# Adaptive modulation products regrouped, and RMS norms applied after the products, in a four-layer fp32 stack

## The reference, cut to what matters

```python
def _rms_norm(x, gain):
    xf = x * lax.rsqrt(jnp.mean(x * x, axis=-1, keepdims=True) + NORM_EPS)
    return xf * gain

def first_block(x, ...):                      # two layers, 512 tokens
    for layer in range(2):
        hn = _rms_norm(x, norm_mix_pre[layer])
        mix = _sparse_attn_conv_mixer(hn, ...) if layer == 0 else _mla_mixer(hn, ...)
        x = x + _rms_norm(mix, norm_mix_post[layer])
        hn = _rms_norm(x, norm_ffn_pre[layer])
        x = x + _rms_norm(jnp.square(jax.nn.relu(hn @ mlp_w1[layer])) @ mlp_w2[layer], norm_ffn_post[layer])

def adaln(cvec, w, b):                        # w is 1024 x 3072
    return jnp.split(jax.nn.silu(cvec) @ w + b, 3, axis=-1)

def second_block(x, c, ctx, c_ctx, ...):      # two layers, 512 + 256 tokens
    for i in range(2):
        shift, scale, gate = adaln(c, mod_w[i], mod_b[i])
        shift_c, scale_c, gate_c = adaln(c_ctx, mod_w[i], mod_b[i])
        u_lat = rms_norm(h_lat, norm_g[i]) * (1.0 + scale) + shift
        u_ctx = rms_norm(h_ctx, norm_g[i]) * (1.0 + scale_c) + shift_c
        ...                                   # i = 0 differential attention, i = 1 neighbourhood attention
        h_lat = h_lat + gate * out_l          # and h_ctx + gate_c * out_c after i = 0
```

## Time and profile before

| | |
|---|---|
| median of 3 runs | 4143.25 us (4135.88 to 4145.75) |
| profiled execution | 4144.13 us, span 4142.5 us |
| PE / DVE / ACT busy | 93% / 50% / 27% of the span |
| mean granted TensorE clock | 0.959 |
| modulation products (L1466) | 768 instructions, 136.2 us |
| MLP products (L456) | 3584 instructions |

### The profile page before, as it was taken

The page is one execution under the profiler, slowest core; times in us unless marked ns, Lnnn a source line. Parts: engine busy times, 40 slices in busy tenths (PEclk is TensorE's granted clock), DMA queues, the critical chain, the costliest instruction groups (busy, mean ns, idle before and its releaser), DMA issues. The chain is left out here.

```text
span 4142.5 us, 44540 instructions
## 1 busy us (share of the span) xinstructions
PE 3833.1 (93%) x16250; PEld 2479.6 (60%) x16250; DVE 2058.4 (50%) x3726; ACT 1136.8 (27%) x2079; POOL 142.6 (3%) x227
## 2 busy tenths in 40 slices
PE   6998999998889999999999999999697999999989
PEld 2445688874445888866565656565354555555554
DVE  3743453533553635446666666666303555555540
ACT  1112100011331000103343444434100444444430
POOL 6500000000000000000000000000000000000000
PEclk8998899987998999889999999999899999999999
DMA  7521323321013332421010111111011121111111
GB/s 151 138 71 46 102 76 97 82 77 48 22 46 88 90 91 72 107 77 36 26 32 29 30 30 30 30 30 31 15 51 46 48 56 56 56 56 56 56 41 53
DMA packets 456432, 246.26 MB, mean 59 GB/s; under 512 B 44256, under 2 KB 448352, under 8 KB 456320
## 3 DMA queue, kind: packets, MB, share of 16 engines
q1 hardware_dynamic: 420384, 216.15, 18.8%
q0 software_dynamic: 14144, 28.36, 2.6%
q10 hardware_dynamic: 21792, 0.22, 0.4%
HBM read 229.83 MB, written 14.80 MB: 59 GB/s over the span
## 5 line engine op out<-in xcount | busy, mean ns | idle before, releaser
L1152 PE MATMUL bank<-hT,ring 128*128 128x512 f32 (+1 forms) x1664 | 634.0, 531 | 23.4 <-DVE hT L1527 19.8
L1628 PE MATMUL bank<-hT,ring 128*128 128x512 f32 (+1 forms) x1536 | 521.1, 491 | 21.0 <-DVE big L1880 16.3
L1152 PEld LDWEIGHTS bank<-hT,ring 128*128 128x128 f32 x1664 | 310.8, 191 | 300.8 <-issue 269.5
L1628 PEld LDWEIGHTS bank<-hT,ring 128*128 128x128 f32 x1536 | 287.4, 190 | 250.3 <-issue 212.5
L326 PE MATMUL bank<-big,ring 128*128 128x512 f32 (+1 forms) x1024 | 391.9, 546 | 12.1 <-DVE big L1892 8.4
L326 PEld LDWEIGHTS bank<-big,ring 128*128 128x128 f32 x1024 | 196.7, 192 | 206.0 <-issue 185.5
L1057 ACT ACTIVATE arena<-bank 128x512 f32<-128x512 f32 (+2 forms) x224 | 118.3, 528 | 461.7 <-PE bank L1050 461.6
L456 PE MATMUL bank<-big,arena 128*128 128x256 f32 x1024 | 228.8, 379 | 0.0
L456 PEld LDWEIGHTS bank<-big,arena 128*128 128x128 f32 x1024 | 194.6, 190 | 26.5
L1025 DVE CUSTOM_DVE_ANT_0 arena<-bank,big 128x512 f32<-128x512 f32 (+2 forms) x152 | 101.3, 666 | 199.7 <-PE bank L1005 199.7
L1623 PEld LDWEIGHTS bank<-ring,hT 128*128 128x128 f32 x1536 | 177.7, 192 | 30.4 <-DVE arena L1847 17.0
(11 more groups left out here) (278 smaller groups left out, 5515.4 us busy)
## 6 DMA issues: line engine op xcount, KB each, us to landing
ring<-in_mlp_w SPq DMA_DIRECT2D x128, 512.0 KB, 5.2
ring<-in_a_w_in SPq DMA_DIRECT2D x64, 512.0 KB, 4.0
ring<-in_b_w_in SPq DMA_DIRECT2D x64, 512.0 KB, 4.0
ring<-in_mod_w SPq DMA_DIRECT2D x48, 512.0 KB, 3.7
ring<-in_even_w_in SPq DMA_DIRECT2D x32, 512.0 KB, 4.0
bias_d<-tb POOLq DMA_DIRECT2D x96, 128.0 KB, 3.4
big<-bias_d POOLq DMA_DIRECT2D x16, 768.0 KB, 5.4
ring<-in_a_w_out SPq DMA_DIRECT2D x16, 512.0 KB, 3.7
```

Of the source, the lines that this page charges most:

```text
L1152: mm = pe.matmul(bk(b + n)[0:m, 0:z - a], ring[s][:, k, 0:m], (rhs or hcol)(k, a, z), start=k == 0, stop=k == kt - 1)
L1628: mm = pe.matmul(flatb[2][:, a:z], ring[s][:, k, :], hT[:, k, a:z], start=k == 0, stop=k == KT - 1)
```

## The change

1. **Modulation.** `cc` grows to 32 columns (30 of zeros) and becomes the stationary operand; four slabs move at a time, each to its own 32 columns of the array and its own 32 partitions of bank 5. 48 blocks are dealt as 8, 4, 4, 8 in each half: 8 in each residual stage, 4 each at steps 7 and 13 of each MLP. The result is copied (`dve_mod_copy`), turned by a transpose (`pe_mod_turn`) and added to the bias (`dve_mod_add`).
2. **Residual stages.** ACT writes `hT = xT * gain` tile by tile behind DVE's additions, and the squares go to another buffer. The reciprocal of the second root moves behind the start of the products.
3. **MLP.** C11, C12 and C21/C22 are evacuated by DVE as `max(x, 0) * rs`, and ACT squares them. `u2` comes ahead of S1 and S2, and S3 ahead of the four differences in an `up` step.
4. **`low`.** DVE evacuates with `* rs`; tables are made behind the second product; the first latent's sums and scaling come behind its own products.
5. **Second block.** The context half is normed in `mlp1` (residual 2 covers 768 tokens, residual 3 only 512) and its shift is on ACT; the latent half is handed over tile by tile, its shift on ACT. The first product of `dif` and of `nat` waits for each tile.
6. **Norm 9.** DVE adds the squares in `wout2`, PE sums once. The first two groups of `nat` start on latent and context halves apart.

```diff
-        MODS = [0, 11, 22, 33, 48]
+        MODS = [("mod0", 0, 8, 0), ("modx0", 8, 4, 0), ("mody0", 12, 4, 4), ("mod1", 16, 8, 0),
+                ("mod2", 24, 8, 0), ("modx1", 32, 4, 0), ("mody1", 36, 4, 4), ("mod3", 40, 8, 0)]
+        MOD_STEP = {7: 1, 13: 2}
-                    mm = pe.matmul(bk(5)[:, 2 * n:2 * n + 2], ring[s][:, k, :], cc[:, k, :],
-                                   start=k == 0, stop=k == KT - 1, skip_group_check=True)
-                mm.then_inc(slab_done[s], 1)
+                    for j in range(4):
+                        mm = pe.matmul(bk(5)[32 * j:32 * j + 32, P * q:P * q + P], cc[:, k, :],
+                                       ring[s0 + 4 * q + j][:, k, :], start=k == 0, stop=k == KT - 1,
+                                       skip_group_check=True)
+                        if k == KT - 1:
+                            mm.then_inc(slab_done[s0 + 4 * q + j], 1)
+            dve.tensor_copy(mod_raw[:, 0:32 * blocks], bk(5)[:, 0:32 * blocks]).then_inc(md_r, 1)
+                m = pe.transpose(bk(5)[:, C + P * q:C + P * q + P], mod_raw[:, P * q:P * q + P], ident)
...
         def sp_mlp(sp, mlp):
             for st in mlp.steps:
+                if st.s - 1 in MOD_STEP:
+                    sp_mod(sp, 4 * mlp.i + MOD_STEP[st.s - 1])
...
         def pe_mlp(pe, mlp):
+                if s == 2:
+                    pe_mod_turn(pe, 4 * mlp.i)
+                if s in MOD_STEP:
+                    pe_mod(pe, 4 * mlp.i + MOD_STEP[s])
+                if s - 1 in MOD_STEP:
+                    pe_mod_turn(pe, 4 * mlp.i + MOD_STEP[s - 1])
...
         def act_mlp(act, mlp):
+                if s == 4 and mlp.i == 1:
+                    act_shifted(act, 0, 1)
-                    act.wait_ge(m_prod, mlp.past("prod") + 7 * s + P2)
-                    act.activation(c11, st.C, ACT.Relu).then_inc(m_c11, 1)
+                    act.wait_ge(m_c11, mlp.past("c11") + s + 1)
+                    act.activation(kept(B11, st.j), c11, ACT.Square).then_inc(m_b, 1)
+                    act.activation(b12, c12, ACT.Square).then_inc(m_b, 1)
+                    act.wait_ge(m_c2, mlp.past("c2") + u + 1)
+                    act.activation(pair, c2.rearrange("p (a n) -> p a n", a=2), ACT.Square).then_inc(m_b, 1)
...
         def dve_mlp(dve, mlp):
             weights(first, S3)
+            dve_rs(dve, mlp.pre, mlp.c)
...
+                done(P6)
+                dve.wait_ge(m_copied, mlp.past("copied") + 2 * s + 1)
+                dve.tensor_tensor(u2, p1s[e], st.X, ALU.add).then_inc(m_u2, 1)
                 if nxt:
                     weights(nxt, S1)
                     weights(nxt, S2)
+                if s == 2:
+                    dve_mod_add(dve, 4 * mlp.i)
+                if s == 3 and mlp.i == 1:
+                    dve_modulated(dve, 0, 1)
+                if s in MOD_STEP:
+                    dve_mod_copy(dve, 4 * mlp.i + MOD_STEP[s])
+                if s - 1 in MOD_STEP:
+                    dve_mod_add(dve, 4 * mlp.i + MOD_STEP[s - 1])
-                    dve.wait_ge(m_c11, mlp.past("c11") + s + 1)
-                    dve.tensor_tensor(kept(B11, j), c11, c11, ALU.mult).then_inc(m_b, 1)
+                    dve.scalar_tensor_tensor(out=c11, in0=st.C, scalar=0.0, in1=rs[:, 0:H],
+                                             op0=ALU.max, op1=ALU.mult).then_inc(m_c11, 1)
...
+            for k in range(KT):
+                act.wait_ge(r_x, KT * r.i + k + 1)
+                if g_pre is not None:
+                    act.activation(hT[:, k, 0:S], xT[:, k, 0:S], ACT.Copy, scale=gains[:, g_pre, k:k + 1])\
+                        .then_inc(n_out, 1)
+                act.activation(sqr[:, k, 0:S], xT[:, k, 0:S], ACT.Square).then_inc(n_sq, 1)
...
-            if g_pre is not None:
-                dve_rs(dve, r.pre, c)
-                dve_scaled(dve, xT, gains[:, g_pre, :], hT, c)
+            dve_mod_copy(dve, (0, 3, 4, 7)[r.i])
...
+                dve.tensor_tensor(lat[:, n, :], bk(n % 2), rs[:, 0:S], ALU.mult).then_inc(l_raw, 1)
+                if n == 1:
+                    dve_tables(dve, tab1, 1)
+                if n == 4:
+                    scaled(0, 0, 3)
...
+        def act_shifted(act, layer, c):
+                act.wait_ge(u_t, base + k + 1)
+                act.activation(hT[:, k, a:z], hT[:, k, a:z], ACT.Identity, bias=mods[:, layer, k, c:c + 1])\
+                    .then_inc((n_out, u_c)[c], 1)
...
+            dve_gated_squares(dve, gated2, pre9)
+            dve_rs(dve, pre9, S)
+            dve_modulated(dve, 1, 0)
+            dve.reciprocal(rs[:, S:TT], rs[:, S:TT]).then_inc(n_rs, 1)
+            dve.wait_ge(n_rs, pre9.i + 2)
+            dve_modulated(dve, 1, 1)
             dve_nat(dve)
```

More of the change, by code:

```diff
@@ L652, in dve_mlp @@
                     dve.tensor_tensor(half_sum[tb_][:, 0:H], u3, st.Z, ALU.subtract).then_inc(m_free, 1)
-                if nxt:
+                if nxt and not st.up:
                     weights(nxt, S3)
@@ L1470, in dve_mod_out @@
[L1470 to L1478 removed]
+            phase, n0, blocks, s0 = MODS[b]
@@ new lines, in dve_mod_copy, with pe_mod_turn @@
+        def dve_mod_copy(dve, b):
+            phase, n0, blocks, s0 = MODS[b]
+            if b == 0:
+                dve.wait_ge(b_w, 16 * 8 * 12)
+            for s in range(blocks):
+                multiplied(dve, phase, s0 + s, 0)
+            dve.tensor_copy(mod_raw[:, 0:32 * blocks], bk(5)[:, 0:32 * blocks]).then_inc(md_r, 1)
+        def pe_mod_turn(pe, b):
+            pe.wait_ge(md_r, b + 1)
+            for q in range(MODS[b][2] // 4):
+                m = pe.transpose(bk(5)[:, C + P * q:C + P * q + P], mod_raw[:, P * q:P * q + P], ident)
+            m.then_inc(md_t, 1)
@@ L1624, in project @@
                                            start=k == 0, stop=k == KT - 1, skip_group_check=True)
+                elif x == "q" and h is None:
+                    for c, (a, z) in enumerate(spans(TT)):
+                        if c:
+                            pe.wait_ge(u_c, KT)
+                        for k in range(KT):
+                            if c == 0:
+                                pe.wait_ge(n_out, res3.pre.k + k + 1)
+                            mm = pe.matmul(flatb[2][:, a:z], ring[s][:, k, :], hT[:, k, a:z],
+                                           start=k == 0, stop=k == KT - 1)
                 else:
@@ L2339, in _ @@
             act_std(act, pre9, TT, 6)
+            act_shifted(act, 1, 0)
+            act_shifted(act, 1, 1)
             run_pairs(nat, "act", act)
```

266 lines of the change are left out of this document (145 added, 121 removed).

## The result

The changed kernel takes 4002.56 us, the median of 4 runs (4002.36 to 4011.99), against 4143.56 (4135.88 to 4145.75): a ratio of 0.9668, 95% interval 0.9650 to 0.9687. That is 141 us less. The profiled execution took 4011.99, span 4010.3; the other three have spans of 4000.7 to 4000.9. The steps are compared by the profiled pair, spans 4142.5 and 4010.3.

A forecast was written before the change was run, and what follows sets the result against it. TensorE, busy 93% of the span, was taken as the bound, with stages one behind another so savings add. Terms -20, -42, -19, -31, -17 and +13 sum to -116 us, taking 4144.1 to 4028; 8-in-10 range 4008 to 4070.

The forecast's parts named there:

- +13: Both MLPs together: 13 us added by modulation visits, transposes, slab waits and ACT's margin, less the saving from u2.
- the one term for `u2`: MLPs: putting u2 ahead of S1 and S2 ends eight TensorE waits, -6.0 us.
- the reserves for a low clock: Residual stages: time allowed for half clock, such as P2 taken at 486 where the chain gave 485.2.
- The visits: MLP steps 7 and 13: four visits of four modulation blocks, 2.5 us each, +10 us.
- The wait at the slab: MLP step 8: slabs requested only after step 7's modulation, delaying C11 and P7; 2.5 us per MLP, +5.
- The margin of ACT: MLP: ACT's new square precedes the copy of P1, leaving 0.1 to 0.2 us before P6; +1, at most 10.
- (a): Modulation: strips don't overlap, so each instruction costs 0.117 us, twice that at half clock; 4092 us, chance 0.08.
- (b): Residual stages: the clock stays at half throughout because TensorE has gaps between short work; 4069 us, chance 0.15.
- (c): MLP hand-overs are tight: ACT late by 0.3 us per `up` step, 5 us at each step 8; 4042, chance 0.17.
- (d): Slower than before: P6 late by over 3.6 us in each of 32 `up` steps; 4156 at 4 us, chance 0.02.
- (e): Per-tile waits of `dif` and `nat` bring nothing, losing half of -31 and of -17; 4052 us, chance 0.05.
- three signs of a wrong forecast: Strip cadence above 0.06 us, clock under 0.6 up to the first steps, or PE waiting for ACT before P6 each step.

The follow-up runs named there:

- e4: Kernel before the change, with only the sum u2 moved ahead of S1 and S2 on DVE; 4124.40 us, ratio 0.9958 to the kernel before.
- e3: Changed kernel with the modulation's inner loops exchanged, so each 32-column strip finishes before the next; 4020.35 us, ratio 0.9710 to the kernel before.
- e2: Changed kernel with the old two-column modulation product (slab stationary) at the new places; 4115.64 us, ratio 0.9938 to the kernel before.
- e10: Changed kernel, but the first products of `dif` and `nat` wait for all eight input tiles; 4018.04 us against 4000.84 for the changed kernel.
- e9_again: Changed kernel timed again without any edit, five runs; 4000.84 us, ratio 0.9684 to the kernel before.
- e6: Changed kernel, but TensorE waits for the norm's reciprocal before each MLP's first product and the low-rank product's first; 4039.30 us against 4010.16.

## Why the prediction was right, and where it was not

The mechanisms were right and the size was not: the median is 25 us below the forecast and 5.4 below the range. The step that failed is the largest mis-sized term of the sum, **+13** for what the MLPs pay; it measured +3.9, and nearly half of the difference is the one term for `u2`, put at -6.0 from a list of waits and measured at -10.2. The second is the reserves for a low clock in the four residual stages, 8.8 us too much together with rounding. With 1.6 the other way in the rest, these two bring 4028 to 4012, still inside the range. The last 9.4 are a difference between executions, for which the range had no room below.

**The mechanisms.** The four residual stages and norm 9 hold to the microsecond where the chain was added up from rows. In residual 0 the chain gave P2 at 485.2; it came 27.73 behind the opening sum, which is 485.1 on the clock of before (457.40 + 27.73). I then took 486. In residual 2 it gave 1328.5, came at 1328.4 (1299.10 + 29.33), and I took 1330.5 in case the sums over 768 tokens ran at half clock. In residual 3 the sums were taken to end at 1759 out of 1757 to 1764 and ended at 1757.0 (1677.1 - 1658.6 = 18.5 behind the opening sum, 1738.5). `low` began 1.4 us earlier than the 915, its tail was 11.5 for 11.6. Norm 9: 24.41 gives 3157.7 for 3157.4. So the stages are short by 1.1 + 2.5 + 2.2 + 3.0 = 8.8 us. Of these 6.2 are my reserves for a low clock (0.8, 1.4, 2.0 and 2.0), where the granted clock over the stage was 0.85 to 0.95, and some 1.7 are rounding of the terms (the chain of residual 3 gave 31.9, and I wrote 31). The modulation of residual 1, put at 10 us for a half clock, took 5.15 at 0.71.

**The MLPs.** The +13 was +3.9, 9.1 us less, and `u2` is nearly half of it. Term by term: `u2` -10.2 for -6.0 (`e4`). The visits: from the timeline of step 7 below, the visit shifts the next product by 567.47 - 563.77 - 1.73 = 1.97 (1.73 is the pace of these products), and that one runs 0.10 longer; 2.07 for 2.5, four of them 8.3 for 10. The wait at the slab is 1.98 in `mlp0` and 1.61 in `mlp1` for 2.5 each, 3.6 for 5. The margin of ACT cost nothing: no wait of PE for it in the stage. What is left, turns, hand-overs and the scaling at step 3, is 390.79 - 383.83 - 4.14 - 1.98 = 0.8 in `mlp0` and 1.3 in `mlp1`, with 0.24 of wait for C11 at step 3. This takes the -10.2 over from the kernel before, where `e4` measured it; in the changed kernel `u2` was not moved back.

```profile
563.77 1.89 PE L466 MATMUL bank<-arena 128*128 128x256 f32 x8
565.59 1.95 PE L1517 MATMUL bank<-ring,cc 128*32 128x128 f32 x64
567.47 1.99 PE L466 MATMUL bank<-hT,ring 128*128 128x256 f32 x8
...
580.08 1.99 PE L466 MATMUL bank<-arena 128*128 128x256 f32 x8 [1.98 <-DVE arena L628]
```

The chain of that wait is the forecast one, from DVE's first wait for the slabs of step 8 to C11 and P7:

```profile
577.40 0.69 DVE L558 TENSOR_TENSOR arena<-ring 128x512 f32<-128x512 f32 x1 [2.89 <-DMA ring<-in_mlp_w]
```

**Modulation.** I took 0.035 us an instruction between 0.027 and 0.117; it is 0.029, with 0.1 for entering the strips and 0.1 on the product behind them in the rows above. I had 0.2 for entering alone, from the earlier trace rows. Both bounds were right, and the value should have been nearer to halving. At two times 0.1 the 16 switches of the kernel, in and out of the strips eight times, are 1.6 us.

**The rivals.** (a), strips don't overlap, is refuted by `e3`, and even there its price would have been 19 us and not 64: in residuals 0 and 2 TensorE had time to spare ahead of the squares, its products cost 0.088 and not 0.117, and during the 11.3 us of them in residual 0 it was granted 1.00. (b), half clock throughout, did not occur: behind the pauses of 2.9 to 8.5 us in these stages the clock fell for a while (0.63 for 4.65 us in residual 0, 0.82 in `dif`'s first product, 0.70 in `nat`'s), and came back each time. Behind those of 1.4 to 2.4 us there it stayed at 1.00 for the 2 us that followed; one of 2.15, in `wout0`, had 0.63 for 4 us. The 0.51 over the 19 us of the earlier trace rows in residual 1 has a pause of 3.80 ahead of it, but TensorE was busy for 18.89 of the 19, and in `e2` two-column products were granted 0.50 with 1.41 as the only pause ahead, and in after, behind the same 3.80, the clock was 0.60 for 4.00 us and 0.97 in the 4.74 that followed: so the gap can account for the start of that stretch and not for its length. (c): a wait of 2.0 and of 1.6 for C11 in the visited step 7, and no wait for ACT in the `up` steps. (d) did not occur. (e) did not occur: PE waits for each tile, and `e10` puts the hand-over by tiles at 4.1 us at `dif` and 2.2 at `nat`, 6.3 and not the 24 that the rival took off.

**The signs.** Of the three signs of a wrong forecast none came (cadence 0.029 to 0.042, granted clock 0.85 and more over each stage, no wait for ACT ahead of P6). They tested the mechanisms, and those held.

**The rest.** -132.2 against -116: 8.8 from the stages, 9.1 from the MLPs, less 0.5 at norm 9 and 1.1 in the other stages. (The sum, too, was taken from the profiled execution: 4144.1 - 116 is 4028.1; from the median it is 4027.3.) That puts the profiled execution, 4011.99, inside the range; the median of the four, 9.4 lower, is outside. Those 9.4 are of the size of the 8.7 by which `e9_again`, the same kernel, is faster ahead of residual 0, at a higher granted clock between 350 and 450 us; the three executions of the median left no trace, so that this is their difference too is likely and not shown. Over all 19 executions the median is 4010.13, inside the range, so that the first median fell below it is in part luck of the draw. My range was built from the terms alone and left no room for it. What sets the clock's course there from one execution to the next is open. The context half normed in `mlp1`, and the order of `low`, were not tried alone, and `e2` and `e6` overlap in the residual stages (14.4 and 8.7 for a gain of 21.1 in residual 0), so their prices don't add up.

## What to carry to other kernels

Products that move few columns cost twice here: by their own time (two columns 0.115 us at best, 128 columns 0.117) and, two columns, by the clock during and behind them (0.50 for both in `e2`). Turned round, with the short side stationary in 32-column strips and the strips interleaved, 64 of them cost 2.1 us between full products. An exact scale by row can stand behind the product; what it buys is what lies ahead of the first consumer of the scale, so count all products up to there. A reserve for a low clock belongs in the range and not in the forecast, since one per stage adds up. A list of waits can leave out short ones, so look at the starts too. And a range needs room for what the same kernel does from one execution to the next.

## What the runs showed of the hardware

Interleaved over four strips, 128x32 products of 128 columns start every 0.029 us at a granted 1.00 (3.70 and 3.73 us for 128 in residuals 0 and 2), and every 0.040 and 0.042 at a granted 0.71 and 0.67 (5.15 and 5.40 us in residuals 1 and 3). In turn it is 0.088 at a granted 1.00 (0.093 in a visit, 5.95/64). Going into the strips and back costs 0.1 us each way (0.09 ahead of them and 1.99 for 1.89 on the product behind, in the visit of step 7).

A product that moves two columns takes 0.115 us at best (1.84 for 16 in residual 0 of before, at a granted 1.00) and 0.213 in residual 1 of before (17.07 for 80, at 0.50). TensorE's granted clock was 0.50 during 18 us (`e2`) and 24 us (`e4`) in which it was busy all the time with two-column products and, in `e4`, sums between them. With strips in turn it was 1.00 during 11.3 us.

One execution of a program on one core differs from the next: the changed kernel took 3998.67 to 4014.92 in 19 executions, the kernel before 4129.69 to 4162.77 in 42. Between two profiled ones 8.7 of 12 us lay ahead of residual 0, with one stretch of 100 us at 0.85 or 0.97. Residual stages of the changed kernel repeat to 0.2 us, norm 9 takes 23.6 or 24.4, and the long stages vary more (`att1` 283.6 to 286.4, `mlp0` 390.3 to 395.1, the rest of `dif` 1321.6 to 1324.0 in its four profiled executions). Residual 0 with two-column products took 48.8 in one and 59.6 in another.
